# Layer block on one core: the last adaLN product moved from the query-weight stage into the value pass, x1 read back in eight pieces

## The reference, cut to what matters

```python
mod = silu(c) @ ada_w + ada_b                    # ada_w: 2048 x 12288, six parts of 2048 columns
shift1, scale1, gate1, shift2, scale2, gate2 = split(mod, 6)
h = rms_norm(x, pre_mix_g) * (1 + scale1) + shift1
y = mixer(h)                                     # pooling and latent attention, then w_out
x = x + gate1 * rms_norm(y, post_mix_g)          # this x is the kernel's x1
h = rms_norm(x, pre_ffn_g) * (1 + scale2) + shift2
q = h @ w_q                                      # 2048 x 2048, the stage "wq"
...                                              # top 16 keys per head and half, 16 experts per head, gates
a = gelu(h @ expert_u.T)                         # all 16384 experts here, "U pass"
y = (a * gates) @ expert_v                       # "V pass"
x = x + gate2 * rms_norm(y, post_ffn_g)
```

## Time and profile before

| | us |
|---|---|
| median of 3 runs | 2148.95 (2148.6 to 2151.83) |
| the profiled execution | 2155.08 |
| its span | 2152.3 |
| PE busy | 1946.9 (90% of the span) |
| DVE busy | 1520.1 (71%) |
| ACT busy | 898.1 (42%) |
| POOL busy | 432.6 (20%) |
| moved by DMA | 436.99 MB, mean 203 GB/s |

### The profile page before, as it was taken

One profiled execution on the slowest core, in us unless ns is written; L12 is line 12 of the kernel. 1 busy time (PEld: TensorE's weight loads), 2 busy tenths in 40 slices (PEclk: granted clock), 3 DMA queues, 4 the chain that ended last, 5 costly groups with the idle time before them and its releaser, 6 DMA issues.

```text
span 2152.3 us, 37807 instructions
## 1 busy us (share of the span) xinstructions
PE 1946.9 (90%) x12388; PEld 1757.5 (82%) x12388; DVE 1520.1 (71%) x2136; ACT 898.1 (42%) x1311; POOL 432.6 (20%) x290
## 2 busy tenths in 40 slices
PE   0489989798999999999999997679999999999995
PEld 0479658698999999999999997568888888888884
DVE  6897489775689999999976667975555555555554
ACT  1143233453334444444444445654444444444443
POOL 1000020000234444444444446840000000000001
PEclk9799859899999999999999999999999999999998
DMA  9989469979567676666677771045555555555553
GB/s 392 414 306 353 157 246 367 295 227 268 131 168 183 180 184 182 180 182 176 175 186 180 184 183 59 0 134 192 192 194 195 194 190 192 194 195 192 190 193 117
DMA packets 227889, 436.99 MB, mean 203 GB/s; under 512 B 23106, under 2 KB 157696, under 8 KB 214016
## 3 DMA queue, kind: packets, MB, share of 16 engines
q1 hardware_dynamic: 226240, 427.84, 63.9%
q0 software_dynamic: 1536, 8.48, 1.0%
q10 hardware_dynamic: 64, 0.02, 0.0%
HBM read 432.04 MB, written 4.21 MB: 203 GB/s over the span
## 4 chain that ended last, share of the span: by engine, by line
PE 79%; DVE 10%; DMA 3%; issue 3%; ACT 2%; DVEq 1%; SPq 1%; POOL 0%; ACTq 0%; POOLq 0%
PE ps L591 14%; PE ps L592 14%; PE ps L593 14%; PE ps L877 11%; PE ps L878 11%; PE ps L880 11%; DVE acc L1229 3%; DVE hotB L1636 2%; DMA ring<-in_ada_w_dram 2%; PE ps L586 2%; DMA i<-consts_dram 1%; DVEq L1636 1%; DVE ring_low L1237 1%; PE ps L568 1%; PE ps L703 1%
## 5 line engine op out<-in xcount | busy, mean ns | idle before, releaser
L591 PE MATMUL ps<-h2H,eH 128*128 128x256 f32 x2048 | 581.5, 284 | 5.8 <-DVE eL L1584 4.5
L592 PE MATMUL ps<-h2L,eH 128*128 128x256 f32 x2048 | 581.0, 284 | 0.0
L593 PE MATMUL ps<-h2H,eL 128*128 128x256 f32 x2048 | 580.9, 284 | 0.0
L1667 DVE TENSOR_TENSOR eL<-raw,eH 128x1024 fp32r<-128x1024 f32 x256 | 313.6, 1225 | 338.2 <-ACT eH L1175 338.2
L1175 ACT CAST eH<-raw 128x1024 fp32r<-128x1024 f32 x256 | 269.9, 1055 | 385.4 <-PE ps L880 379.8
L496 POOL TENSOR_TENSOR eL<-raw,eH 128x1024 fp32r<-128x1024 f32 x128 | 311.4, 2433 | 572.9 <-ACT eH L1101 572.9
L877 PE MATMUL ps<-eH,aH 128*128 128x512 f32 x1024 | 399.2, 390 | 3.6 <-DVE eL L1667 3.6
L591 PEld LDWEIGHTS ps<-h2H,eH 128*128 128x128 f32 x2048 | 394.6, 193 | 6.7 <-DVE eL L1584 5.2
L878 PE MATMUL ps<-eL,aH 128*128 128x512 f32 x1024 | 398.9, 390 | 0.0
L593 PEld LDWEIGHTS ps<-h2H,eL 128*128 128x128 f32 x2048 | 394.7, 193 | 0.0
L592 PEld LDWEIGHTS ps<-h2L,eH 128*128 128x128 f32 x2048 | 394.6, 193 | 0.0
(11 more groups left out here) (254 smaller groups left out, 2313.1 us busy)
## 6 DMA issues: line engine op xcount, KB each, us to landing
raw<-in_peer_u_dram SPq DMA_DIRECT2D x1024, 128.0 KB, 3.0
raw<-in_peer_v_dram SPq DMA_DIRECT2D x256, 512.0 KB, 3.4
ring<-in_ada_w_dram SPq DMA_DIRECT2D x48, 2048.0 KB, 19.9
ring<-in_w_out_dram SPq DMA_DIRECT2D x8, 2048.0 KB, 11.9
ring<-in_peer_wq_dram SPq DMA_DIRECT2D x32, 512.0 KB, 15.5
ring<-in_w_in_dram SPq DMA_DIRECT2D x6, 2048.0 KB, 14.7
ring<-in_w_uq_dram SPq DMA_DIRECT2D x2, 1536.0 KB, 9.0
ring<-in_w_in_dram SPq DMA_DIRECT2D x2, 1280.0 KB, 11.7
```

The lines of the kernel that those rows point to most:

```text
L591: pe.matmul(o, lh, rh, start=start, stop=False, skip_group_check=True)
L592: pe.matmul(o, lh, rl, start=False, stop=False, skip_group_check=True)
L593: return pe.matmul(o, ll, rh, start=False, stop=stop, skip_group_check=True)
L1667: dve.tensor_tensor(eL[:, slot, :], raw[:, slot, :], eH[:, slot, :].bitcast(F32), ALU.subtract).then_inc(v_lo, 1)
```

## The change

Part 5 leaves the ring. In `load_order` the eight wq entries now stand alone, so six of them lie in the ring at once. DVE's 32 steps between the `weight_low` calls, `ada_columns(5, 3)`, `gate_column(1, ...)`, `gate_rows(1, 3)` and `gate_out(1, 3)` go.

In the V pass, `ada_w`'s last 2048 columns come in 16 pieces of 1 MB (128x2048, one row of `ada_w` for each partition). SP issues the first three behind the U pass, POOL the other thirteen, each when the piece three back is used up. DVE does one step of 128x1024 (`last_gate`) behind each of the V tiles 3 to 34, then, behind tile 35, transposes the sums in blocks of 32x32 (128x2048), and behind tile 38 reduces them over 32 neighbours to 128x64. POOL brings the four quarters to 32 partitions, adds them and stores the 2048 sums to DRAM with one element to a descriptor. POOL then loads `x1` in eight pieces of 256 KB, one each four tiles from tile 48 on, spreads the sums over all partitions (`gate2`), and loads bias and gain spread in the same way; DVE adds and multiplies them behind tiles 89 and 104 (`gate_row`). The tail is as before. Two of the thirteen small vector loads at the start go.

```diff
-            + between + mixed(wout, 4) + mixed(wq, 5) + [("keys", 0, 0)])
+            + between + mixed(wout, 4) + wq + [("keys", 0, 0)])
...
+        def load_piece(eng, k):
+            eng.dma_start(piece[k % 3][:], ada_v[:, k, 5 * D:6 * D]).then_inc(piece_done(k)[0], 16)
...
             for j in range(RING):
                 sp.dma_start(raw[:, j, :], vb[j // 2, j % 2]).then_inc(v_in[j], 16)
+            sp.wait_ge(u_used, 2 * TILES)
+            for k in range(3):
+                load_piece(sp, k)
...
-            pool.wait_ge(row_stored, 32)
+            for k in range(3, KT):
+                pool.wait_ge(piece_step, 2 * (k - 2))
+                load_piece(pool, k)
+
+
+            pool.wait_ge(quarter_ready, 1)
+            for q in range(4):
+                pool.dma_start(quarters[0:QUAD, q, :], quarter[q * QUAD:(q + 1) * QUAD, :]).then_inc(quarters_in, 16)
+            pool.wait_ge(quarters_in, 64)
...
+            pool.dma_start(gate_dram[1].rearrange("(b l) -> l b", l=QUAD), half2[0:QUAD, 2, :],
+                           allow_slow_non_contiguous=True).then_inc(row2_stored, 16)
             pool.wait_ge(x1_stored, 16)
-            pool.wait_ge(u_used, 2 * TILES)
-            pool.dma_start(x1[:], x1_dram.rearrange("t p d -> p t d")).then_inc(tail_in, 16)
-            pool.dma_start(gate2[:], gate_dram[1:2, :].broadcast_to([P, D])).then_inc(tail_in, 16)
-            pool.wait_ge(tail_in, 32)
+            for i in range(8):
+                pool.wait_ge(v_used, 2 * (48 + 4 * i))
+                cols = slice(i % 4 * W, (i % 4 + 1) * W)
+                pool.dma_start(x1[:, i // 4, cols], x1_dram[i // 4, :, cols]).then_inc(tail_in, 16)
+            pool.wait_ge(row2_stored, 16)
+            pool.dma_start(gate2[:], gate_dram[1:2, :].broadcast_to([P, D])).then_inc(gate2_in, 16)
...
-            ada_columns(5, 3)
             for i in range(ROUND):
                 u_tile(0, i, i < 3)
-            gate_rows(1, 3)
...
             u_round(0, first=True)
-            gate_out(1, 3)
...
                         weight_low("wq", n, j)
-                    ada(1)
...
             u_round(0, first=True, pairs=False)
-            gate_column(1, 5, 3, V_B5, V_PO2)
...
-            with dve.Fori(1, TILES // 3) as r:
+            def last_gate(step):
+
+                k, h = step // 2, step % 2
+                if h == 0:
+                    dve.wait_ge(*piece_done(k))
+                a, w = (t[:, h * 1024:(h + 1) * 1024] for t in (sums2, piece[k % 3]))
+                if k == 0:
+                    dve.tensor_scalar(a, w, c_act[:, 0:1], None, ALU.mult).then_inc(piece_step, 1)
+                else:
+                    dve.wait_ge(piece_step, step - 1)
+                    dve.scalar_tensor_tensor(a, w, c_act[:, k:k + 1], a, ALU.mult, ALU.add).then_inc(piece_step, 1)
...
+            for tile in range(3, 36):
+                v_tile(tile, tile % 3, False)
+                if tile < 35:
+                    last_gate(tile - 3)
+            dve.wait_ge(piece_step, 2 * KT)
+            dve.transpose(sums2[:], sums2[:]).then_inc(sums_turned, 1)
+            for tile in range(36, 39):
+                v_tile(tile, tile % 3, False)
+            dve.wait_ge(sums_turned, 1)
+            dve.tensor_reduce(quarter[:], sums2[:].rearrange("p (b l) -> p b l", l=QUAD), AX_X,
+                              ALU.add).then_inc(quarter_ready, 1)
```

More of the change, by code:

```diff
@@ L209, in hybrid_block @@
     gate2 = at("gate2", M + 4096, [D])
+    piece = [at(f"piece{i}", M + 2048 * i, [D]) for i in range(3)]
+    sums2 = at("sums2", M + 6144, [D])
+    quarter = at("quarter", S + 1712, [KT * 4])
+    quarters = at("quarters", M + 6144, [4, KT * 4])
+    half2 = at("half2", M + 6400, [3, KT * 4])
+    extra = at("extra", M + 6144, [D])
     raw = at("raw", M + 8192, [RAW, HF])
@@ L468, in _ @@
             pool.dma_start(quad_rows(V_B4), quads(ada_b[0, 4 * D:5 * D])).then_inc(vrow_in, 16)
[L469 removed]
+            for m, v in enumerate((ada_b[0, 2 * D:3 * D], post_mix_g[0])):
                 pool.dma_start(vrow2[m * KT:(m + 1) * KT, :], rows(v)).then_inc(vrow_in, 16)
@@ L1671, in _, with gate_row @@
                 v_tile(j, j, True)
-            with dve.Fori(1, TILES // 3) as r:
+            def last_gate(step):
[8 more added lines that the diff above has]
+                    dve.scalar_tensor_tensor(a, w, c_act[:, k:k + 1], a, ALU.mult, ALU.add).then_inc(piece_step, 1)
+            def gate_row(i, op):
+                dve.wait_ge(gate2_in, 16)
+                dve.wait_ge(extra_in, 16 * (i + 1))
+                dve.tensor_tensor(gate2[:], gate2[:], extra[:], op).then_inc(gate2_ready, 1)
+            for tile in range(3, 36):
[9 more added lines that the diff above has]
+                              ALU.add).then_inc(quarter_ready, 1)
+            with dve.Fori(13, 30) as r:
+                for j in range(3):
+                    v_tile(r * 3 + j, j, False)
+            gate_row(0, ALU.add)
+            with dve.Fori(30, 35) as r:
+                for j in range(3):
+                    v_tile(r * 3 + j, j, False)
+            gate_row(1, ALU.mult)
+            with dve.Fori(35, TILES // 3) as r:
                 for j in range(3):
```

36 lines of the change are left out of this document (26 added, 10 removed).

## The result

| | before | changed |
|---|---|---|
| first comparison, median | 2150.39 us (2148.60 to 2156.68, 4 runs) | 2135.06 us (2130.29 to 2136.15, 4 runs) |
| its ratio, 95% interval | | 0.9919 [0.9897, 0.9941] |
| second comparison, median | 2152.35 us (2147.65 to 2156.91, 21 runs) | 2132.53 us (2131.09 to 2133.55, 5 runs) |
| its ratio, 95% interval | | 0.9903 [0.9884, 0.9921] |

By medians the change gains 15.3 us in the one and 19.8 us in the other; by the ratios it is 0.8 to 1.0%. The forecast was 27.5 us, 2121.5 us, range 2116 to 2131. So the direction was right and the size was not. The profiled execution of the changed kernel took 2130.29 us, the shortest of its four.

The account below looks back on a forecast made before the run. PE was taken to bound the kernel (79% of the span), with gaps in wq and early U. Gains 18.7 + 3.5 + 5.3 = 27.5 us, V at no cost, off 2148.95 gave 2121.5 us, range 2116 to 2131.

Parts of the forecast that it names:

- Part A: Stage wq: without the ada_w loads most PE waits and clock falls go, 113.4 to 94.7 us, gain 18.7 us.
- I take no fall: Stage wq: PE's clock does not fall after the remaining first wait of 2.4 us; 3.2 us kept for the range.
- rival 1: Clock still falls at wq's first wait, U's start, or both: 3.2 and 1.6 us less gain, 2123 to 2126; chance 0.18.
- The row of 520 to 530 us: Stage wq before: clock stayed at 1.00 with 2.84 us idle spread over that stretch; taken as evidence against a fall.
- that can only be clock: Stage wq before: 9.6 us, 99.8 us of busy PE less 90.2 of pace, put down to half clock.
- B: Start of the U pass: the one-column sums go and tile 0 ends at 569.0 instead of 572.5; gain 3.5 us.
- C: Seventh U tile: without the gate's row the wait and the slow stretch behind it go; gain 5.3 us.
- Part D: V pass: DVE's 32 steps, the transpose and the added transfers stay within cover of low parts and loads; cost 0.
- rival 4: V pass: 4-byte writes are dear, showing from 0.19 us each; at 0.41 all gain goes, about 2149; chance 0.02.
- end hundreds of us before the tail: 0: V pass: transposed sums, the four quarters and the loads of bias and gain finish early and cost nothing.
- Rival 2: V pass: loads late beside pieces plus a DVE step reach PE, 3 to 18 us, 2125 to 2140; chance 0.10.
- The tail, "0": End of the program: the tail, with the two small loads gone at the start, was to change the time by 0.

Follow-up runs that it names:

- the run with the loads alone: Changed kernel with the eight 2 MB loads of the last ada part put back between wq's loads, read by nobody: 2148.66 us, ratio 0.9981.
- the one with the steps alone: Changed kernel with 32 extra DVE steps of 128x1024 between the low parts of wq, without any load: 2136.67 us, ratio 0.9925.

## Why the prediction was wrong

**Part A, 18.7 us, was the step that failed.** Its mechanism was right, as the run with the loads alone and the one with the steps alone show. Its size was off by three terms.
- *The base.* The sum took the stage's 113.4 us from one profile. The mean of five is 110.3, so the stage had 3.1 us less to give.
- *The clock.* "I take no fall" failed in the profile on record and in four of the six others that have this stage unchanged; the other two had a shorter wait, 1.4 and 1.6 us. That was rival 1. The row of 520 to 530 us could not settle it, nor could the length of the wait: the clock stayed at 1.00 behind 2.41 us in one profile and behind 3.39 in another. The price was wrong too, 1.4 to 1.7 us instead of 3.2. The 9.6 us "that can only be clock" held 1.4 us of pace, and the falls were not alike: the first of them cost 2.7 us, twice what the one in the changed kernel did.
- *The pace.* 91.6 us of busy PE, not 90.2: the three pairs at `qT` and the two ends of the stage were left out.

The last two terms are the measured 97.7 less the forecast 94.7, 3.0 us, of which some 1.7 are clock and 1.4 pace. Together 18.7 - 3.1 - 3.0 = 12.6, and 110.3 - 97.7 is 12.6.

**The starting point.** The prediction took its gain off 2148.95, the median of three runs, having noted that the profiled execution lay 6.1 us above it. Over the 21 runs of the second comparison the kernel before has a median of 2152.35. So more than half of the 6.1 us was that the three runs were short ones. The other 2.7 was a profile longer than usual, and the stages that the change shortens had their part in it: wq was 3.1 us above its mean, and what follows up to the last gelu 0.8. With the same 27.5 us the forecast from 2152.35 would have been 2124.9, still 7.7 us below the 2132.5 measured beside it.

**Parts B and C were right for the profile on record.** Together they were 8.6 us between the two profiles, 8.8 forecast. B: the gelu of tile 4 starts 45.0 us behind the end of wq before and 41.5 after, 3.5 us. C: from tile 4 to tile 6 it is 16.8 us before and 11.6 after, 5.2 us. No one-column matmul stands before U, and no wait at the seventh tile. But 1.5 us of C were a fall of the clock that two of four profiles of before do not have, and against their mean (761.7 us from wq's end to the last gelu) B and C give 7.9.

**Part D, "cost 0", was nearly right and for a good reason, with two leaks.** The pieces and the 32 steps cost PE nothing. The cover (the time by which the low parts are ready ahead of PE) was there, and the doubled steps show that little of it is left. V's loads took 4.9 us in the median, where 3.3 to 4.6 on average were expected, and ACT waited for 18 of them, but none of it reached PE while the pieces ran. The transpose and the reduce took 2.3 us each and reached nobody. The leaks are the small transfers behind them:
- *The store with 4-byte descriptors*, 1.3 us. Its price was spread over V's whole stream: 128 descriptors a DMA engine against 19 us of idle time. But they stand in the queues in one burst. 10.8 us to landing for 128 of them is at most 0.08 us each, four times the 18 ns of the earlier trace rows and less than half of the 0.19 from which rival 4 was to show. The three loads of V issued beside the burst took 7.0 to 9.9 us instead of 3.3, and cover of 5.5 us was not enough. The Trainium skill, "DMA: Bandwidth & Descriptors", rules for kernel authors, says that a strided last dimension lowers to one descriptor per element and should be made contiguous; this case's trace agrees, with 10.8 us against 4.5. The same page of the Trainium skill, in its specifications, names 512 B as the least size without a read-modify-write; here runs of 128 bytes, a quarter of that, already cost PE nothing.
- *Gate, bias and the last part of x1 together*, 1.4 us. The text had them "end hundreds of us before the tail: 0". It asked when they were needed, not what they stood beside.

Rival 2 named this mechanism, loads late beside other transfers, but at the pieces, and counted 3 us at the least. The pass grew by 3.4 us, but not there: 2.7 are these two gaps, from transfers that it didn't name, and 0.7 lie within what the V pass of before varies by (697.5 to 698.4 in five profiles).

**The tail, "0", was wrong by 2.0 us** and could not be read from any row of before: POOL's transfers had cost nothing there that showed.

**The whole.** Against what a usual execution of before holds: wq 12.6, U 7.9, less 2.7 in V (700.7 in a usual profile of after, 698.0 of before) and 2.0 at the end, is 15.8 us; the runs gave 15.3 and 19.8. What the mixer adds between the two kernels, if anything (its means lie 2.0 us apart, in a spread of 6), stays open.

## What to carry to other kernels

A sum made on one profile must be made against the stage's usual length: where the profiled execution lies above the median, ask whether the median rests on enough runs, and look whether the surplus is in what the change removes, or take the profile again. Small transfers beside a stream that has a few microseconds of cover should have contiguous runs and stand apart from one another; ask of each not only when it is needed but which loads it delays. And an engine has room for extra work up to the cover of the one that follows it: here one step of 1.28 us a tile cost nothing, a second one 12.5 us.

## What the runs showed of the hardware that I had not expected

- Each transfer that POOL issues adds 0.08 us to the end of the program, whatever its size: from the last store's issue to the end 6.7 us with 19 transfers, 7.0 with 23, 8.2 with 37, 8.7 with 44, 9.0 with 47. Transfers moved to ACT's queue did not count (the kernel with 23).
- A store of 2048 numbers with 4 bytes to a descriptor took 10.8 us to land, with 128 bytes 4.5 us. The former delayed other loads (7.0 to 9.9 us instead of 3.3) enough to cost PE 1.3 to 2.8 us each time.
- At one place of the program, the granted clock fell behind nine of eleven waits of 2.3 to 3.4 us, and stayed at 1.00 behind the other two (2.41 and 3.39 us) and behind waits of 1.4 and 1.6 us. A fall cost 1.4 to 1.7 us in the changed kernel, and 2.7 in the first profile of before.
- The same code of before took 107.9 to 113.4 us in the stage that is bound by its loads, and the changed one 95.4 to 97.9.
